# Expert stage of a two-layer encoder trunk: one-hot gather and add-back as fp32r products of high and low parts

## What is computed

```python
def moe_swiglu(h, w_router, b_router, w_up, w_down):
    b_, s, d = h.shape
    t = h.reshape(b_ * s, d)
    logits = (t @ w_router).astype(jnp.float32) + b_router.astype(jnp.float32)
    top_vals, top_idx = lax.top_k(logits, TOP_K)
    weights = jax.nn.softmax(top_vals, axis=-1)
    combine = jnp.sum(jax.nn.one_hot(top_idx, N_EXPERTS, dtype=jnp.float32) * weights[..., None], axis=1)
    out = jnp.zeros_like(t)
    for e in range(N_EXPERTS):
        out = out + combine[:, e:e + 1].astype(t.dtype) * swiglu(t, w_up[e], w_down[e])
    return out.reshape(b_, s, d)
```

## Time and profile before

| What | Value |
|---|---|
| Median of 3 runs | 1881.16 us (1880.9 to 1881.74) |
| Profiled execution: its span (first to last instruction) | 1878.5 us |
| Around the span, against the median | 2.7 us |
| Busy, PE / DVE / ACT / POOL | 1657.3 / 1489.8 / 1044.7 / 272.2 us |
| Mean granted TensorE clock | 0.949 |
| Read from memory | 496.66 MB, 265 GB/s over the span |

### The profile page before, as it was taken

The page is one execution under the profiler, slowest core; times in us unless marked ns, Lnnn a source line. Parts: engine busy times, 40 slices in busy tenths (PEclk is TensorE's granted clock), DMA queues, the critical chain, the costliest instruction groups (busy, mean ns, idle before and its releaser), DMA issues.

```text
span 1878.5 us, 22572 instructions
## 1 busy us (share of the span) xinstructions
PE 1657.3 (88%) x7672; PEld 1338.6 (71%) x7672; DVE 1489.8 (79%) x1580; ACT 1044.7 (56%) x1010; POOL 272.2 (14%) x167
## 2 busy tenths in 40 slices
PE   1777776999869897859999999999999999999995
PEld 0766665777657775647778878878788788787883
DVE  5377956688696776678889889799798898897986
ACT  0442223444334443337777777777777776776773
POOL 0348264213232222400000000000000000000000
PEclk9997877999889998969999999999999999999997
DMA  8451332687664555439999999999999999999992
GB/s 275 149 179 46 115 132 90 222 286 270 230 224 144 185 188 215 164 118 316 375 313 346 363 332 363 349 332 381 315 348 363 332 357 354 332 376 335 332 357 109
DMA packets 347594, 498.48 MB, mean 265 GB/s; under 512 B 8504, under 2 KB 271952, under 8 KB 347536
## 3 DMA queue, kind: packets, MB, share of 16 engines
q1 hardware_dynamic: 343888, 489.90, 76.2%
q0 software_dynamic: 1856, 6.01, 1.1%
q10 hardware_dynamic: 1792, 1.83, 0.3%
HBM read 496.66 MB, written 1.05 MB: 265 GB/s over the span
## 4 chain that ended last, share of the span: by engine, by line
PE 66%; DVE 8%; issue 8%; POOL 3%; ACT 1%; DVEq 0%; POOLq 0%; ACTq 0%
PE bank L706 20%; PE bank L708 20%; PE bank L707 20%; DVE acc L1517 3%; PE bank L1098 2%; PE bank L1111 1%; POOL w_part L2137 1%; PE bank L1118 1%; DVE arena L2063 1%; DVE hs L1597 1%; DVE w_part L1557 1%; PE bank L702 0%; DVE small L1603 0%; ACT w_part L1231 0%; POOL mod L2151 0%
## 5 line engine op out<-in xcount | busy, mean ns | idle before, releaser
L1568 DVE TENSOR_TENSOR w_lo<-ring,w_hi 128x2048 fp32r<-128x2048 f32 x338 | 772.1, 2292 | 130.9 <-ACT w_hi L1437 124.4
L1437 ACT ACTIVATE w_hi<-ring 128x2048 fp32r<-128x2048 f32 x336 | 641.4, 1915 | 142.2 <-PE bank L708 132.2
L706 PE MATMUL bank<-w_lo,heT_hi 128*128 128x512 f32 x896 | 359.4, 401 | 2.0 <-issue 1.8
L708 PE MATMUL bank<-w_hi,heT_hi 128*128 128x512 f32 x896 | 350.5, 391 | 0.0
L707 PE MATMUL bank<-w_hi,heT_lo 128*128 128x512 f32 x896 | 349.8, 390 | 0.0
L1231 ACT ACTIVATE w_part<-ring 128x1024 fp32r<-128x1024 f32 (+1 forms) x162 | 168.9, 1049 | 272.6 <-PE bank L708 254.7
L1557 DVE TENSOR_TENSOR w_part<-ring,w_part 128x1024 fp32r<-128x1024 f32 (+1 forms) x105 | 128.7, 1248 | 162.8 <-ACT w_part L1231 162.8
L706 PE MATMUL bank<-w_part,hT_hi 128*128 128x512 f32 (+1 forms) x448 | 181.3, 405 | 24.5 <-POOL w_part L2137 16.7
L2137 POOL TENSOR_TENSOR w_part<-ring,w_part 128x1024 fp32r<-128x1024 f32 (+1 forms) x57 | 139.6, 2454 | 418.5 <-ACT w_part L1231 395.5
L706 PEld LDWEIGHTS bank<-w_lo,heT_hi 128*128 128x128 f32 x896 | 168.3, 188 | 35.8 <-DVE w_lo L1568 2.2
L708 PEld LDWEIGHTS bank<-w_hi,heT_hi 128*128 128x128 f32 x896 | 168.2, 188 | 35.7
(11 more groups left out here) (340 smaller groups left out, 2046.8 us busy)
## 6 DMA issues: line engine op xcount, KB each, us to landing
ring<-in_moe_w_up SPq DMA_DIRECT2D x226, 1024.0 KB, 7.6
ring<-in_moe_w_down SPq DMA_DIRECT2D x112, 1024.0 KB, 6.9
ring<-in_cond_w SPq DMA_DIRECT2D x24, 2048.0 KB, 8.6
ring<-in_ffn_w_up SPq DMA_DIRECT2D x22, 1024.0 KB, 7.7
ring<-in_od_w_in SPq DMA_DIRECT2D x8, 2048.0 KB, 7.8
ring<-in_ev_w_in SPq DMA_DIRECT2D x5, 2048.0 KB, 7.6
ring<-in_ffn_w_down SPq DMA_DIRECT2D x5, 2048.0 KB, 7.6
ring<-in_od_w_in SPq DMA_DIRECT2D x8, 1024.0 KB, 6.5
```

The source lines that it names most:

```text
L706: mm(bank, lhs[0], rhs[1], start=start, stop=False)
L708: return mm(bank, lhs[0], rhs[0], start=False, stop=stop)
L1437: f(w_hi[:, (n + 2 * late) % 3], w[:, half * PIECE:(half + 1) * PIECE], ACT.Copy) \
L1568: tt(w_lo[:, buf], at, w_hi[:, buf].bitcast(F32), ALU.subtract).then_inc(S["w_lo"], 1)
```

## The change

The tokens `hs` are split once, before the stage, into `hs_hi` (ScalarE) and `hs_lo` (GpSimd, in place of `hs`). A one-hot matrix holds only zeros and ones, so it has no low part: `gather` multiplies `hs_lo` and `hs_hi` with `p_tok` in fp32r. The routing weight leaves the turned matrix: ScalarE copies the sign of the turned bank to `back_pT`, VectorE sums the bank's rows to a column `back_w`, one weight per slot, and the copies out of the down banks multiply by it: `ye_hi` on ScalarE with the column as scale, `ye_lo` on VectorE as bank x column - `ye_hi`. `back` multiplies both with `back_pT`. Tiles are laid over others (`overlay` is moved up for it), which adds no instruction.

```diff
+        hs_lo, = overlay(0, ("hs_lo", [P, NT, D], F32R))
+        hs_hi, ye_lo, back_pT = overlay(3 * D, ("hs_hi", [P, NT, D], F32R), ("ye_lo", [P, 2, 512], F32R), ("back_pT", [P, NT, P], F32R))
+        ye_hi, = overlay(8 * D, ("ye_hi", [P, 2, 512], F32R))
...
+        p_tok, = overlay(MOE_AT + 4 * 256 + NT * P, ("p_tok", [P, NT, P], F32R))
...
-        e_s, e_a = er(2, 256), er(2, 256)
-        p_tok, pw_tok = er(NT, P), er(NT, P)
-        pwT = mod[:, 4096:4096 + SEQ].rearrange("p (t s) -> p t s", t=NT)
-        ye = acc
+        e_s, e_a, pw_tok = er(2, 256), er(2, 256), er(NT, P)
+        back_w = mod[:, 4 * D + NT * P:4 * D + NT * P + 1]
@@ TensorE
-                            last = mm(bank[:, j * P:(j + 1) * P], hs[:, t, k * P:(k + 1) * P], p_tok[:, t],
-                                      start=(t == 0), stop=(t == NT - 1))
+                            for part in (hs_lo, hs_hi):
+                                last = mm(bank[:, j * P:(j + 1) * P], part[:, t, k * P:(k + 1) * P], p_tok[:, t],
+                                          start=(t == 0 and part is hs_lo), stop=(t == NT - 1 and part is hs_hi))
...
+            pe.wait_ge(S["tok_all_lo"], NT)
...
-                    mm(bank[:], pwT[:, i // 2], ye[:, i % 2], start=True, stop=True).then_inc(full, 1)
+                    mm(bank[:], back_pT[:, i // 2], ye_lo[:, i % 2], start=True, stop=False)
+                    mm(bank[:], back_pT[:, i // 2], ye_hi[:, i % 2], start=False, stop=True).then_inc(full, 1)
@@ ScalarE
+            for t in range(NT):
+                act.wait_ge(S["h_ready"], 4 * 3 + 2 * t + 2)
+                f(hs_hi[:, t], hs[:, t], ACT.Copy).then_inc(S["tok_all_hi"], 1)
...
-                        take(("pwT",), pwT, lambda b: b[:, 0:SEQ].rearrange("p (t s) -> p t s", t=NT))
+                        bank, _ = item_filled(act, it, "pwT")
+                        f(back_pT[:], bank[:, 0:SEQ].rearrange("p (t s) -> p t s", t=NT), ACT.Sign).then_inc(S["back_pick"], 1)
...
+                item_taken(act, it, "pwT")
                 for h in range(2):
-                    take(("down", h), ye[:, h], lambda b: b[:])
+                    bank, _ = item_filled(act, it, "down", h)
+                    f(ye_hi[:, h], bank[:], ACT.Identity, scale=back_w).then_inc(S["back_hi"], 1)
@@ VectorE
-                        item_filled(dve, it, "pwT")
+                        bank, free = item_filled(dve, it, "pwT")
+                        dve.wait_ge(S["back_pick"], it + 1)
+                        nc.vector.tensor_reduce(back_w, bank[:, 0:SEQ], AX.X, ALU.add).then_inc(free, 1)
...
+                for h in range(2):
+                    bank, free = item_filled(dve, it, "down", h)
+                    dve.wait_ge(S["back_hi"], it * 2 + (h + 1))
+                    stt(ye_lo[:, h], bank[:], back_w, ye_hi[:, h].bitcast(F32), ALU.mult, ALU.subtract).then_inc(free, 1)
@@ GpSimd
-            filled(pool, "hT", 4, 3)
-            nc.gpsimd.memset(pwT, 0.0).then_inc(S["back_zero"], 1)
-            nc.gpsimd.memset(ye[:], 0.0).then_inc(S["back_zero"], 1)
+            for t in range(NT):
+                for half in range(2):
+                    filled(pool, "hT", 4, 2 * half + t)
+                pool.wait_ge(S["tok_all_hi"], t + 1)
+                tt(hs_lo[:, t], hs[:, t], hs_hi[:, t].bitcast(F32), ALU.subtract).then_inc(S["tok_all_lo"], 1)
+            for a in (back_pT, ye_hi, ye_lo):
+                nc.gpsimd.memset(a[:].bitcast(F32), 0.0).then_inc(S["back_zero"], 1)
```

More of the change, by code:

```diff
@@ L258 @@
     "od_rope od_gate ret_var ret_rstd ret_y route_in route_exp rank_in over_ready p_ready e_silu w_hi w_lo w_lo_pool "
-    "turn_hi rows_hi nw_hi nw_lo zeroed piece_used act_hi tok_hi back_zero out_done "
+    "turn_hi rows_hi nw_hi nw_lo tok_all_hi tok_all_lo back_pick back_hi zeroed piece_used act_hi tok_hi back_zero out_done "
     "dve_step last_step pool_step"
@@ L282, in trunk, with overlay @@
         banks = [ctx.enter_context(nc.psum_tensor(f"bank{i}", [P, 512], F32)) for i in range(8)]
+        def overlay(at, *specs):
+            made = []
+            with ExitStack() as place:
+                if at:
+                    place.enter_context(nc.sbuf_tensor(f"before_{specs[0][0]}", [P, at], F32))
+                for name, shape, dt in specs:
+                    made.append(place.enter_context(nc.sbuf_tensor(name, shape, dt)))
+            return made
         ring = sb("ring", [P, RING * UNIT])
         xs = sb("xs", [P, NT, D])
+        hs_lo, = overlay(0, ("hs_lo", [P, NT, D], F32R))
+        hs_hi, ye_lo, back_pT = overlay(3 * D, ("hs_hi", [P, NT, D], F32R), ("ye_lo", [P, 2, 512], F32R), ("back_pT", [P, NT, P], F32R))
+        ye_hi, = overlay(8 * D, ("ye_hi", [P, 2, 512], F32R))
         hs = sb("hs", [P, NT, D])
@@ L298, in trunk @@
         over_int = sb("over_int", [1, 4], I32)
[L300 to L308, removed]
         W_AT, LO_AT, OWN_AT, TRIG_AT = 2 * D, 2 * D + 2 * BUFS * PART, 4 * D + 2 * BUFS * PART, ARENA - 2 * NT * NFREQ
@@ L417, in trunk @@
         assert 2 * P + 8 * P <= N_FIRST - NFREQ
-        er, mt = carver(arena[:, MOE_AT:]), carver(mod[:, 0:4096])
-        e_s, e_a = er(2, 256), er(2, 256)
-        p_tok, pw_tok = er(NT, P), er(NT, P)
-        pwT = mod[:, 4096:4096 + SEQ].rearrange("p (t s) -> p t s", t=NT)
-        ye = acc
+        er, mt = carver(arena[:, MOE_AT:]), carver(mod[:, 0:D])
+        e_s, e_a, pw_tok = er(2, 256), er(2, 256), er(NT, P)
+        assert MOE_AT + 4 * 256 + 2 * NT * P <= ARENA
+        back_w = mod[:, 4 * D + NT * P:4 * D + NT * P + 1]
         ysum = arena[:, 0:W_AT].rearrange("p (t n) -> p t n", t=NT)
@@ L1174, in _ @@
                 taken(pe, "gather", half)
-            pe.wait_ge(S["back_zero"], 2)
+            pe.wait_ge(S["back_zero"], 3)
             with pe.Fori(0, NE) as it:
@@ L1425, in item @@
             def item(it, late=0):
-                def take(key, to, view, func=ACT.Copy):
-                    bank, free = item_filled(act, it, *key)
-                    f(to, view(bank), func).then_inc(free, 1)
                 def split_unit(u):
```

## The result

The changed kernel takes 1898.85 us (median of 4 runs, 1897.68 to 1905.31) against 1881.03 (4 runs, 1879.65 to 1881.74): a ratio of 1.0102, with an interval of 1.0088 to 1.0116. It is 17.8 us slower; the forecast was 1896.9. The profiled execution took 1899.09 us, with a span of 1897.3.

A forecast was written before the change was run, and what follows sets the result against it. TensorE's own stream was taken as the bound, with one hole per expert ended by VectorE's chain. 7 x (0.5 + 2.0) + 0.2 - 2.0 = 15.7 us, added to the 1881.2 median, gave 1896.9 us, range 1883 to 1908.

The forecast's parts named there:

- The hole: TensorE's wait before unit 0's activations' transpose, ended by VectorE's chain, grows from 1.48 to 3.6 us in seven experts.
- The chain's growth: Scaled down-bank copies on ScalarE (0.1) and VectorE's reduction (0.4) lengthen the path by 0.5 us per expert, ends 0.35 and 0.75.
- The clock: Behind the longer hole TensorE's clock falls to half at most experts, costing 2.0 us each, ends 0 and 3.2.
- length alone doesn't decide: TensorE's clock was lost around an idle 2.36 us but held around 3.10, so a hole's length doesn't settle it.
- The hidden pieces: VectorE's two ye_lo (1.4 us) fit its idle 2.33 us; ScalarE's Sign copy is done before VectorE needs it.
- The gather: 32 fp32r products of 128 columns replace 32 fp32 passes: no change, ends 1.6 us gain and 3.6 loss per expert.
- Its rivals, slower and faster: Gather products at 0.21 us each give 1923 us, chance 0.10; at 0.07 each 1887 us, chance 0.07.
- The end and the first expert: The last add-back saves 2.0 us, ends 1 and 3.2; the first expert's 0.4 us hole becomes 0.2 longer.
- The step that failed: Before the experts, the added hs_hi copies, hs_lo subtractions and larger memset cost nothing, up to 0.5 us.
- The sum: Over the whole kernel, 7 x (0.5 + 2.0) + 0.2 - 2.0 = 15.7 us slower.
- The other side: VectorE's chain moves forward with TensorE, so add-back savings count in every expert: 1866.5 us, chance 0.08.

The follow-up runs named there:

- e3: The changed kernel with every pair of add-back products done twice, the first pair thrown away; 1892.25 us, ratio 1.0051 to the kernel before.
- e2: The kernel before with only the add-back half of the change, the gather still fp32; 1899.91 us, ratio 1.0081 to the kernel before.
- e5: The changed kernel with hs_lo made by VectorE instead of GpSimd; 1895.35 us, ratio 1.0066 to the kernel before.
- e4: The kernel before with ScalarE's hs copies and GpSimd's subtractions added, their result unused; 1885.37 us, ratio 1.0010.
- e1: The kernel before with only the gather half of the change, the add-back still fp32; 1887.28 us, ratio 1.0027.
- e7: The kernel before with only the add-back half, Silu and unit 0's product put first, reduction in unit 1; 1866.28 us, ratio 0.9917.
- e9: The kernel before, only reordered: Silu and unit 0's product ahead of pwT's copy and the additions, build later; 1871.62 us, ratio 0.9951.
- e8: The whole change, reordered: Silu and unit 0's product first, reduction in unit 1, build in unit 14; 1870.36 us, ratio 0.9944 to the kernel before.
- e6: The changed kernel with VectorE's build moved from unit 0 to the first down-projection unit; 1882.47 us, ratio 0.9998 to the kernel before.

## Why the prediction was right, and where it wasn't

**The hole.** Forecast 1.48 + 1.6 + 0.5 = 3.6 us; measured 3.70 from start to start, less the product's 0.23, 3.47, seven times, ended by VectorE's product each time. The chain's growth was 0.43 (the period with the full clock) for the 0.5 forecast: the reduction 0.33 for 0.4, and the rest ScalarE's scaled copies for the 0.1 forecast (0.69 us for the second one against 0.60 in the earlier trace rows). e3 confirms it with the clock held.

**The clock.** Forecast 2.0 per expert, at most of them. It fell behind six of seven. The seven periods grew by 15.4 us, so 2.2 each instead of 2.5, and without the chain's 0.4 the clock took 1.8 each. Falls of 3.4 us cost 1.3 to 1.6 and those of 6.8 cost 2.6 to 2.7: as forecast about 0.2 us for each product of 512 columns in them, 14 of these in the window of 6.8. That the average came near 2.0 is in part luck, since with the same holes the clock fell seven times for 6.8 us in e2 and three times for 3.4 in e5. The step "length alone doesn't decide" was the careful one.

**The hidden pieces.** The two ye_lo took 1.40 us and VectorE was idle for another 1.11 before its w_lo, so their cover held. The Sign copy was never waited for.

**The gather.** Forecast no change. In the loop it stayed: from the first to the last of 32 products 3.4 us, and 3.5 before, also the earlier trace rows. The group of the second expert's gather, after:

```profile
L1101 PE MATMUL bank<-p_tok,hs_lo x16: 222/274/276, 1063.6 to 1066.9; 128*128 128x128 f32 x16
```

and before:

```profile
L1098 PE MATMUL bank<-arena,hs x32: 272/275/275, 1056.0 to 1059.5; 128*128 128x128 f32 x32
```

Its rivals, slower and faster, both fell. That the weight load sets the pace of both forms, the prediction's reason, no run tests. The count of passes in the Trainium skill, page "FP8 and Floating Point Precision", TensorE Precision Notes, would have halved it; these rows don't follow it. With 512 columns, in the add-back, an fp32 product took 2 x 0.43 us and an fp32r product 0.23, about the page's four to one; with 128 columns it was 2 x 0.11 against 0.11.

**The end and the first expert.** Forecast 2.0 saved at the end, measured 2.5. The first expert was forecast 0.2 longer and was 1.5 shorter. Its hole became 1.26 us longer and the add-back 1.6 shorter, which gives 0.3; the rest is small waits for w_lo that it no longer had, which were not followed one by one.

**The step that failed** is "Both engines have idle time there, and the gather starts only after the routing: nothing, up to 0.5." It cost 7.3 us. Idle time of GpSimd was no cover, since its subtraction stretched the very VectorE instructions that the routing waits for (3.3 us: e4). And the clock, low since ahead of the routing, was not given back during the fp32r gather: from its start to the first add-back it took 13.3 us before, 17.3 after and 17.2 in e1, which has the fp32 add-back; e4, as late but with the fp32 gather, took 15.0, of which 1.7 go to its second fall. Why the form matters stays open. The forecast asked what the gather takes at the full clock and didn't ask at which it would run.

**The sum.** Forecast 15.7, measured 18.7 between the spans and 17.8 between the medians. The loop with its ends gave 11.4 of it, 4.3 less than forecast; the head added 7.3. The two misses have opposite signs, so the time came out nearer than the terms were.

**The other side.** That the change could win, by 14.7 us, had 0.08, "if Silu were what VectorE waits for". Nothing of it happened in this order. Once the order was changed too, the add-back half won about half its size (e7, 8.1 us from the mark against e9), and in e8 the head took nearly all of it back.

## What to carry to other kernels

Before saving time on an engine, look at what ends its next wait: if that is another engine's chain, the saving makes the wait longer, and a longer wait on TensorE can also lose the clock. From the mark the add-back half cost 19.8 us in the old order and, against the kernel before in the same new order, saved 8.1. And compare like with like: the whole change in the new order is 11 us faster than the kernel before, but so is, within 1 us or so, the kernel before with the new order alone. Idle time on GpSimd was not free here, because VectorE had two-input work on the path beside it.

## What the runs showed of the hardware that was not expected

- After a wait of 3.31 us on TensorE, the granted clock fell for 6.8 us seven times out of seven (e2), for 3.4 or 6.8 us in six of seven (the change, the same six in two executions), and for 3.4 us in three of seven (e5). After 1.3 to 1.5 us it never fell, 7 of 7 in each of before, e1, e3, e4 and e6. In e6 it fell once in seven during a gather that came 0.6 us late.
- A gather of 32 fp32r products with 128 columns ran at 0.22 us each at the low clock (830.99, 831.21, 831.42 in the changed kernel) and the full clock did not come in the 7 us that it took, in eight profiles of eight; the same gather in fp32 passes did within 5.5 us, in five of five. Both read as fully busy in the windows, so the records don't say what tells them apart. In e6 the clock was lost during such a gather. At the full clock both forms held it in the other gathers inside the stage.
- Two subtractions of 128x1024 on GpSimd took 3.09 and 4.38 us beside VectorE's two-input work, where 55 of the same shape elsewhere took 2.5 on average, and one VectorE step of 0.18 took 1.9.
- A ScalarE copy of 128x512 from a bank with a scale from memory took 0.68 us on average (16 of them), against 0.59 without, to fp32r as to f32.
